# Time mixer of a hybrid decoder block: a block inverse with one product a level, and six runs of small products a period

## The reference

```python
def rwkv7_scan(r, w, k, v, kk, a):
    def step(S, inp):
        r_t, w_t, k_t, v_t, kk_t, a_t = inp
        sa = jnp.einsum('bhij,bhj->bhi', S, -kk_t)
        S = (S * w_t[:, :, None, :]
             + sa[..., None] * (kk_t * a_t)[:, :, None, :]
             + v_t[..., None] * k_t[:, :, None, :])
        y_t = jnp.einsum('bhij,bhj->bhi', S, r_t)
        return S, y_t
```

## Time and profile before

| | |
|---|---|
| median of three executions | 2472.08 us (2471.37 to 2472.72) |
| span of the profiled execution | 2469.5 us, so 2.6 us less than that median; its own time outside the span is not recorded apart |
| time mixer with the input projection | about 60 to 710 us of the span |
| pooling, merge and output projection | about 710 to 1250 us |
| expert layer | about 1250 us to the end |
| PE, DVE, ACT busy over the span | 2193.7, 1533.5 and 727.0 us |

### The profile page before, as it was taken

One profiled execution on the slowest core, in us unless ns is written; L12 is line 12 of the kernel. 1 busy time (PEld: TensorE's weight loads), 2 busy tenths in 40 slices (PEclk: granted clock), 3 DMA queues, 4 the chain that ended last, 5 costly groups with the idle time before them and its releaser, 6 DMA issues.

```text
span 2469.5 us, 39419 instructions
## 1 busy us (share of the span) xinstructions
PE 2193.7 (89%) x16183; PEld 1536.9 (62%) x16183; DVE 1533.5 (62%) x2579; ACT 727.0 (29%) x1383; POOL 664.8 (27%) x541
## 2 busy tenths in 40 slices
PE   7999999999999999999989888988787787777776
PEld 6899999999989999988644444533332232222222
DVE  7777777787764554456855776677445544444445
ACT  4555555555434444342211111111111000000000
POOL 1000000000000000002555545555545445444442
PEclk9999999999999999999999999999999999999999
DMA  5433333333347666484999999999999999999997
GB/s 198 137 94 86 100 88 89 97 90 86 97 120 224 184 187 182 139 303 181 404 420 423 423 426 427 427 427 428 427 427 427 426 427 427 427 427 427 427 427 290
DMA packets 346278, 708.29 MB, mean 287 GB/s; under 512 B 13834, under 2 KB 270434, under 8 KB 279778
## 3 DMA queue, kind: packets, MB, share of 16 engines
q0 software_dynamic: 74176, 537.01, 51.7%
q1 hardware_dynamic: 271684, 168.55, 23.3%
q10 hardware_dynamic: 240, 0.22, 0.0%
HBM read 703.63 MB, written 2.10 MB: 286 GB/s over the span
## 4 chain that ended last, share of the span: by engine, by line
DMA 33%; PE 15%; DVE 2%; issue 2%; POOL 1%; DVEq 0%; ACT 0%; POOLq 0%; ACTq 0%
DMA down_rows<-in_v_table,experts 25%; PE bank L1695 11%; DMA up_rows<-in_u_table,experts 8%; PE bank L1611 2%; POOL down_rows L1599 1%; DVE up_rows L1811 0%; PE bank L1638 0%; PE bank L1653 0%; PE bank L1659 0%; ACT diagonal L1755 0%; DVE one_hot L1251 0%; DVE expert_sides L1257 0%; PE bank L1621 0%; PE bank L1665 0%; DVE side_index L1230 0%
## 5 line engine op out<-in xcount | busy, mean ns | idle before, releaser
L1695 PE MATMUL bank<-down_rows,diagonal 128*128 128x512 f32 x2032 | 947.7, 611 | 210.7 <-DMA down_rows<-in_v_table,experts 173.1
L1811 DVE CUSTOM_DVE_ANT_0 up_rows<-up_rows,h 128x2048 f32<-128x2048 f32 x256 | 585.2, 2292 | 523.2 <-DMA up_rows<-in_u_table,experts 523.2
L1695 PEld LDWEIGHTS bank<-down_rows,diagonal 128*128 128x128 f32 x2032 | 375.2, 193 | 741.9 <-issue 385.7
L1593 POOL DMA_INDIRECT up_rows<-in_u_table,experts x256 | 286.0, 1117 | 1207.2 <-POOLq L1269 1091.4
L1599 POOL DMA_INDIRECT down_rows<-in_v_table,experts x256 | 370.3, 1446 | 523.5 <-PE bank L1695 510.5
L182 DVE TENSOR_TENSOR w_half_rest<-w_half,w_half_high 128x1024 fp32r<-128x1024 f32 x224 | 273.0, 1221 | 180.8 <-ACT w_half_high L161 178.9
L197 PE MATMUL project<-hT_high,w_half_high 128*128 128x272 f32 (+1 forms) x1152 | 353.5, 307 | 1.6 <-DVE r L909 1.3
L197 PE MATMUL project<-hT_high,w_half_rest 128*128 128x272 f32 (+1 forms) x1152 | 330.6, 287 | 0.0
L197 PE MATMUL project<-hT,w_half_high 128*128 128x272 f32 (+1 forms) x1152 | 330.0, 287 | 0.0
L161 ACT CAST w_half_high<-w_half 128x1024 fp32r<-128x1024 f32 x224 | 234.7, 1051 | 191.3 <-PE merge_ps L197 122.0
L197 PEld LDWEIGHTS project<-hT_high,w_half_high 128*128 128x128 f32 x1152 | 216.9, 188 | 11.3 <-DVE r L909 1.5
(11 more groups left out here) (338 smaller groups left out, 3013.2 us busy)
## 6 DMA issues: line engine op xcount, KB each, us to landing
w_half<-in_w_in SPq DMA_DIRECT2D x176, 512.0 KB, 4.0
w_half<-in_w_branch_a SPq DMA_DIRECT2D x32, 512.0 KB, 3.9
out_w<-in_w_out SPq DMA_DIRECT2D x16, 1024.0 KB, 5.3
query_w<-in_w_q_peer SPq DMA_DIRECT2D x10, 1024.0 KB, 19.7
w_half<-in_w_branch_b SPq DMA_DIRECT2D x16, 512.0 KB, 3.8
out_w<-in_w_q_peer SPq DMA_DIRECT2D x6, 1024.0 KB, 29.5
up_rows<-in_u_table,experts POOLq DMA_INDIRECT x256, 21.1
down_rows<-in_v_table,experts POOLq DMA_INDIRECT x256, 20.5
```

The lines of the kernel that those rows point to most:

```text
L1593: pool.indirect_dma_start(ur[n % RU][:], None, w["u_table"][0], bass.IndirectOffsetOnAxis(ap=k.idx[:, t, h, j:j + 1], axis=0)).then_inc(s_ ...
L1695: mm = nc.tensor.matmul(acc[t][c][:], dg[n % RD][:], vr[n % RV][:, quarter(c)], start=(n == 0), stop=(n == last(t, c)), skip_group_check=True)
L1811: v.tensor_tensor_reduce(ur[n % RU][:], ur[n % RU][:], k.h[:, n // (HEADS * TOPK), :], 1.0, 0.0, ALU.mult, ALU.add, dots[:, n:n + 1]).then ...
```

## The change

The carry of the inverse is changed. The mask of `LT_diag` becomes strict (`s < t`). `Y` and a transposed `L X` (`lx`) lie side by side in one tile `Y_LX_blocks`. Unit `Z 1` makes L X once; DVE transposes it into `lx`. From then on, levels 1 to 3 multiply `Z_st` by both at once, 64 columns, and DVE adds the result to both, transposes `lx` into `X_blocks` and masks that into the next `Z_st` itself. Units `Z 2`, `Z 3` and `Z 4` are gone. The last level (`T 5`) becomes `Tl 5` and moves from the end of a period, ahead of 18 `f`, to the start of the next. `ORDER` is written anew: `s 0`, `Z 1`, `r 1`, `t 1`, `T 1`, `u 1` and `lw` stand in one run, `la` comes three `f` after `lw`, and the 48 `f` are dealt out over fewer gaps.

```diff
-    c[:, C_LEV:C_LEV + CH] = s // HALF == t // HALF
+    c[:, C_LEV:C_LEV + CH] = (s // HALF == t // HALF) & (s < t)
...
-    ("r", 0), ("gr", 0), ("sp", 1), ("t", 0), ("rb", 0), ("u", 0), ("t", 1), ("Z", 0), ("s", 0), ("sp", 2), ("f", 2),
-    ("lw", 0), ("f", 4),
...
+    ("Tl", 5), ("r", 0), ("gr", 0), ("sp", 1), ("t", 0), ("rb", 0), ("u", 0), ("Z", 0), ("sp", 2), ("f", 6),
+    ("s", 0), ("Z", 1), ("cv", 0), ("r", 1), ("t", 1), ("T", 1), ("u", 1), ("lw", 0), ("f", 3), ("la", 0), ("f", 4),
...
+CARRIED = (1, 2, 3)
...
-        xs, yb = (sb(n, [P, NCH, HALF]) for n in ("X_blocks", "Y_blocks"))
+        xs, yz = sb("X_blocks", [P, NCH, HALF]), sb("Y_LX_blocks", [P, 2, NCH, HALF])
+        yb, lx = yz[:, 0], yz[:, 1]
...
                 for c in chunks(i):
-                    mm = by_head(inv[1][:, c * HALF:(c + 1) * HALF], zs[:, c, :], yb[:, c, :])
+                    if i in CARRIED:
+                        mm = by_head(inv[1][:, c * CH:(c + 1) * CH], zs[:, c, :], yz[:, :, c, :])
+                    else:
+                        mm = by_head(inv[1][:, c * HALF:(c + 1) * HALF], zs[:, c, :], yb[:, c, :])
...
-                wait(dve, q["Z"], p * 5 + i)
+                wait(dve, q["Z"], p * 2 + (1 if i == 1 else 2))
+                n0 = chunks(i).start
+                if i == 1:
+                    n.transpose(flat(lx), inv[2][:, 0:NCH * HALF])
+                expand(i, c3(inv[2][:, n0 * HALF:NCH * HALF], HALF))
...
+                if i in CARRIED:
+                    both = inv[1][:, 0:TP].rearrange("p (c b t) -> p b c t", b=2, t=HALF)
+                    n.tensor_tensor(yz[:], yz[:], both, ALU.add).then_inc(q["Y"], 1)
+                    d()
+                    n.transpose(flat(xs), flat(lx))
+                    d()
+                    expand(i + 1, xs[:, chunks(i + 1).start:, :])
+                    return
```

More of the change, by code:

```diff
@@ L501 @@
          "gr": 2, "rb": 2, "lo": 2, "Z": 2, "T": 2, "yf": 2, "t": 2,
-         "r": 3, "u": 3, "s": 3, "yc": 3, "gv": 3, "ge": 3, "gy": 3}
+         "Tl": 3, "r": 3, "u": 3, "s": 3, "yc": 3, "gv": 3, "ge": 3, "gy": 3}
 WINDOWS_AT = ((1, 0), (1, 2))
 GATES = 4
+CARRIED = (1, 2, 3)
 STREAM = ("ahead", "sp", "f", "e")
@@ L670, in gr @@
                 wait(pe, q["kst"], p + 1)
-                wait(pe, q["Y"], p * LEVELS)
+                wait(pe, q["Zst"], p * 5)
                 wait(pe, q["off"], p)
@@ L679, in rb @@
                 wait(pe, q["rst"], p + 1)
+                wait(pe, q["Y"], p * LEVELS)
                 for n, lhs in enumerate((bst, kst)):
@@ L702, in Z @@
                     return
-                wait(pe, q["X"], p * 5 + i)
+                wait(pe, q["X"], p * 2 + (1 if i == 1 else 2))
                 if i == LEVELS - 1:
@@ L759, in _ @@
             schedule({"f": f, "lw": lw, "la": la, "lg": lg, "nm": nm, "bo": bo, "gr": gr, "rb": rb, "t": t,
-                      "Z": Z, "T": T_, "r": r_, "u": u_, "s": s_, "gv": gv})
+                      "Z": Z, "T": T_, "Tl": T_, "r": r_, "u": u_, "s": s_, "gv": gv})
             f(2 * KT, PAIRS + 3, 0)
@@ L843, in lo @@
             def lo(_, p, par):
-                wait(act, q["Z"], p * 5)
+                wait(act, q["Z"], p * 2)
                 wait(act, q["maskT"], p + 1)
@@ L970, in Z, with expand @@
                     return
-                wait(dve, q["Z"], p * 5 + i)
+                wait(dve, q["Z"], p * 2 + (1 if i == 1 else 2))
[3 more added lines that the diff above has]
+                expand(i, c3(inv[2][:, n0 * HALF:NCH * HALF], HALF))
+            def expand(i, z):
                 c0 = chunks(i).start
-                z = inv[2][:, c0 * HALF:NCH * HALF].rearrange("p (c b t) -> p c b t", b=1, t=HALF).to_broadcast((P, NCH - c0, 2, HALF))
+                z = z.rearrange("p c (b t) -> p c b t", b=1).to_broadcast((P, NCH - c0, 2, HALF))
                 level = k.const[:, C_LEV + CH * i:C_LEV + CH * (i + 1)].rearrange("p (c b t) -> p c b t", c=1, b=2).to_broadcast((P, NCH - c0, 2, HALF))
@@ L1033, in _ @@
             schedule({"ahead": sp_, "sp": sp_, "cv": cv, "e": e, "la": la, "nr": nr, "bo": bo, "ab": ab, "gr": gr, "rb": rb,
-                      "Z": Z, "T": T_, "r": r_, "s": s_, "ge": ge, "gy": gy})
+                      "Z": Z, "T": T_, "Tl": T_, "r": r_, "s": s_, "ge": ge, "gy": gy})
             window(6)
```

## The result

The changed kernel takes 2513.93 us (median of four, 2513.37 to 2514.50) against 2471.86 us: ratio 1.0169, 95% interval 1.0155 to 1.0183. It is slower by 42 us; forecast were 2517 us, in 2495 to 2540.

A forecast was written before the change was run, and what follows sets the result against it. It took PE's own pace to bound the time mixer (busy 643 of 650 us): 5.35 us of new waits less 2.3 us spared, 3.0 us a period, 45 us over 15 periods, gave 2517 us, range 2495 to 2540.

The forecast's parts named there:

- Both sums per period: PE in a time mixer period: 2.3 us less work and waiting, against 5.35 us of new waits.
- `la`: Between `lw` and `la`, PE waits 0.95 us for ACT's table load and activation, with only three `f` between.
- Chunk 2: PE waits about 1.8 us for the state: 0.4 uncovered, the rest because DVE is on the weights' half.
- Chunk 3: PE waits 0.8 us for the state: a later cast and half on DVE, with the uncovered 0.42.
- Chunk 4: PE waits 0.4 us, only the uncovered state.
- Chunk 1: PE waits 1.2 us at `Z 1` and the state, behind DVE's last-level addition and the weights' half `sp 2`.
- `T 1` and `rb`: PE waits an estimated 0.2 us directly behind what DVE has to do for them.
- the rival of half pace: `T` with a two-block 64-column operand at half pace: 1.7 us more a period, 2543 us; chance 0.06.
- The clock: Sign of a wrong prediction: PE's granted clock below 1.00 because of the new waits, costing on every product.
- The table load: Rival at `la`: a load of twice its 1.28 us makes `la` wait 1.28 us longer, 2536 us; chance 0.02.
- Only latencies remain: Rival: halves never in the way, waits 0.95 at `la` and 0.42 at four states, about 2476 us; chance 0.06.
- Faster, with the table load hidden: Rival: ACT loads its table before the decay product ends, `la` does not wait, 2463 us; chance 0.05.

The follow-up runs named there:

- experiment 1: The changed kernel with one unit moved: the weights' half `sp 3` behind `s 1` instead of between `la` and chunk 2's state; 2488.94 us, ratio 1.0074.
- experiment 2: The changed kernel with `T 2`, `T 3`, `T 4` each put ahead of `r 2`, `r 3`, `r 4`; 2493.18 us, ratio 1.0089 to the kernel before.
- experiment 3: The changed kernel with `la` moved past three `f`, so six `f` behind `lw`; 2532.74 us, ratio 1.0250 to the kernel before.
- experiment 5: The changed kernel with both `la` six `f` behind `lw` and the half `sp 3` behind `s 1`; 2492.28 us, ratio 1.0086 to the kernel before.
- experiment 4: The new inverse under the order of the kernel before, with only `Z 2` to `Z 4` struck; 2465.15 us, ratio 0.9974 to the kernel before.
- experiment 6: The new inverse under the order before, without `Z 2` to `Z 4`, and `T 2` to `T 4` ahead of `r 2` to `r 4`; 2448.64 us, ratio 0.9907.
- experiment 8: The new inverse under an order written for it, halves behind the states and `T 5` ending the 18 `f`; 2429.80 us, ratio 0.9832 to the kernel before.

## Why the prediction was right

- **Both sums per period held.** New waits, read from start to start in the rows above, against the forecast: `la` comes 2.64 us behind `lw` (619.90 to 622.54), a wait of 1.05 (0.95 forecast). Chunk 2: 1.8 (1.8). Chunk 3: 0.89 less 0.14, 0.75 (0.8). Chunk 4, where 0.56 us pass from the `MT_st` product to the state's: 0.4 (0.4). Chunk 1: 0.74 for S and 0.23 for X ahead of `Z 1` (616.40 to 616.75 less 0.12), 0.97 (1.2). `T 1` and `rb`: 0.1 (0.2). In sum 5.1 us, where 5.35 were forecast. The period grew by 2.77, so by the difference 2.3 us were spared, as forecast.
- **The largest term, chunk 2, had the mechanism right**: experiment 1 moves one half and nothing else, the wait there falls from 1.8 to 0.42 us, and 25 us are gone.
- **The 64 columns cost nothing**, 0.59 us for ten products; the rival of half pace fell.
- **The count of periods was too simple, and came out nearly right, in part by luck.** The sum was 3.0 us for 15 periods, 45 us; measured were 42. By the decay products, the last comes 40.1 us later than before (660.1 against 620.0 us). The twelve full gaps make 33 us of it at 2.77 each. The first three gaps and what lies ahead of them make only 3.5 and not 9, since there only part of the units run. Another 3.5 lie in four longer gaps (42.04, 40.51, 40.31 and 41.38 us), most of it the lowered clock, which the sum had at nothing. Up to the start of the merge 1.7 us more come after the last decay product.
- **One wait was in no term.** The last level now stands at the head of the next period (`Tl 5`), and in one period behind the last decay product DVE does 3.0 us of work of the pooling branch (`pool_in` and `r`, 726.04 to 729.04) between PE's products of that level and its own addition. PE waits for `Y_st` there, 3.2 us, once. The kernel before has no such wait. Experiments 1, 2, 3 and 5, with the same `Tl 5`, have it too, all at 3.2 us; 4, 6 and 8, where the level is `T 5` at the end of a period, do not.

```profile
729.38 0.43 PE L575 MATMUL chain<-rhs,Y_st 64*64 64x64 f32 x4 [3.24 <-DVE Y_st L1008]
```

- **The clock was named as what would prove the prediction wrong, and it did fall**, three times in the mixer of the profiled execution, though for little. At 343.8 us it fell right behind the wait at chunk 2 (2.0 us of idle there), at 507.6 us 1.5 us behind one, and at 729.5 us beside the wait for `Y_st`. The rows of before gave no sign of it because they have no such wait; the step that failed is to take that for a reason that it would not happen.
- **The table load** took 1.28 us again (620.71). The Trainium skill, page "ScalarE: Activation LUTs", section "Table sets: the hidden batching unit", gives some 2.7 us for a switch. The trace does not agree: the activation began 1.29 us after the load did (622.00), and by the row the wait at `la` came out right.
- **The rivals.** "Only latencies remain" needed every half out of the way. Experiment 1 moves one, and chunk 2 then waits 0.42 us as the rival had it; but chunk 1 still waits 0.98 and chunk 3 0.77 us, with a half ahead of each, so that it stayed at 2489 us and not at 2476. "Faster, with the table load hidden" did not happen: ACT began the load 0.81 us behind `lw`'s start.

## What to carry to other kernels

Before a product is removed from a full engine, look at what it stood in front of: its time is a gain only where nothing behind it was being waited for. Here ten products of 0.56 us covered 0.42 us of a state's latency, and a saving of 2.3 us a period became a loss of 2.8 until the remaining work was dealt out anew, and then a gain of 2.3. In kernels whose engines share one order written by hand, read for each wait which instruction stands ahead of the awaited one on its own engine: one 1.2 us piece of stream work there cost 25 us of 2514.

## What the runs showed of the hardware

A wait can cost more than its length. In experiment 3 PE idled for 2.26 us (once 2.63) at the state of chunk 2 in each of 14 periods, and at 13 of these waits the granted clock fell from 1.00 to 0.50, mostly for 3.4 us; at the one of 310.9 us it stayed. At the same place in the change it fell behind the one wait of 2.02 us and behind one of the 13 of 1.65, in experiment 2 behind the one wait of 1.44 us and behind none of the 13 of 1.07, and with 0.8 us or less (experiments 1 and 5) it stayed at 1.00 in all full periods. So the same wait can bring a fall or not, and the longer ones did so more often. Experiments 4 and 6 had one fall each in the mixer, at 116 and 119 us, behind waits of 1.42 and 1.26 us; experiment 1 has one of 1.25 us there and no fall. What else sets off the fall was not tried. Moving `la` made this kernel 19 us slower although PE idled no longer by it: 4.0 us in the period of 40.24 us, as in that of the change (40.17 less 36.21).
